# Two transformer blocks on one core: experts' rows leave through DRAM and come back by index on GpSimd

## What is computed

```python
def moe_swiglu(x, w_router, w_gate, w_up, w_down):
    logits = xt @ w_router
    top_vals, top_idx = lax.top_k(logits, 2)
    probs = softmax(top_vals)
    combine = sum(one_hot(top_idx, 8) * probs[..., None], axis=1)
    for e in range(8):
        acc = acc + combine[:, e] * swiglu(xt, w_gate[e], w_up[e], w_down[e])
    return acc

x = layer_norm(ALPHA * x + moe_swiglu(x, ...), ln2_g, ln2_b)
```

## Time and profile before

| | |
|---|---|
| median of 3 runs | 1999.91 us (1999.88 to 2001.02) |
| profiled execution: first to last instruction (span) | 1997.8 us |
| PE busy | 1971.7 us (99%) |
| DVE busy | 1586.5 us (79%) |
| ACT busy | 1226.4 us (61%) |
| POOL busy | 98.7 us (5%) |
| mean granted TensorE clock | 0.998 |
| weights of the experts | 384 transfers of 704 KB |

### The profile page before, as it was taken

How to read it: one execution, slowest core, us unless ns; L and a number is a source line. 1 busy time by engine, 2 the same in 40 slices (tenths; PEclk the granted TensorE clock), 3 DMA queues, 4 the chain that set the end, 5 groups by cost and what they waited for, 6 DMA issues and landing times.

```text
span 1997.8 us, 30577 instructions
## 1 busy us (share of the span) xinstructions
PE 1971.7 (99%) x11807; PEld 1679.3 (84%) x11807; DVE 1586.5 (79%) x1630; ACT 1226.4 (61%) x1323; POOL 98.7 (5%) x163
## 2 busy tenths in 40 slices
PE   8999999999999999999999999999999999999997
PEld 6888888888888898888889888888888888888886
DVE  7787745868774579776658878999999899999997
ACT  6665534566553457455536537777777777777775
POOL 0400000040000000000000000000000000000000
PEclk9999999999999999999999999999999999999999
DMA  8326555632655555075545209999999999999995
GB/s 302 120 90 212 190 190 179 217 117 95 206 190 190 184 201 168 3 236 190 190 169 196 101 19 388 362 362 366 365 358 368 360 366 365 364 364 363 366 361 199
DMA packets 154089, 481.08 MB, mean 241 GB/s; under 512 B 14608, under 2 KB 41728, under 8 KB 153856
## 3 DMA queue, kind: packets, MB, share of 16 engines
q1 hardware_dynamic: 150064, 465.46, 64.7%
q0 software_dynamic: 3920, 14.16, 2.0%
HBM read 477.48 MB, written 2.10 MB: 240 GB/s over the span
## 4 chain that ended last, share of the span: by engine, by line
PE 91%; DVE 6%; ACT 1%; DMA 1%; issue 1%; POOL 1%; SPq 0%; DVEq 0%; POOLq 0%; ACTq 0%
PE G L707 16%; PE G L709 16%; PE G L708 16%; PE Sp L707 5%; PE Sp L709 5%; PE Sp L708 5%; PE G L1212 3%; PE G L734 3%; PE G L1511 3%; PE G L1213 2%; PE G L694 1%; DVE ring_lo L2251 1%; PE G L1512 1%; PE G L689 1%; PE G L690 1%; PE Sp L1212 1%
## 5 line engine op out<-in xcount | busy, mean ns | idle before, releaser
L2174 ACT ACTIVATE e_hi<-e_raw 128x1408 fp32r<-128x1408 f32 x384 | 523.8, 1381 | 156.4 <-DMA e_raw<-in_moe_w_gate 64.2
L3043 DVE TENSOR_TENSOR e_lo<-e_raw,e_hi 128x1408 fp32r<-128x1408 f32 x384 | 601.9, 1620 | 20.1 <-ACT e_hi L2174 17.6
L2251 DVE TENSOR_TENSOR ring_lo<-ring,ring_hi 128x2048 fp32r<-128x2048 f32 (+2 forms) x171 | 383.5, 2254 | 183.2 <-ACT ring_hi L1714 181.8
L1714 ACT ACTIVATE ring_hi<-ring 128x2048 fp32r<-128x2048 f32 (+1 forms) x179 | 335.5, 1883 | 227.5 <-PE G L709 109.7
L707 PE MATMUL G<-e_hi,xgTh 128*128 128x512 f32 (+1 forms) x768 | 289.2, 377 | 0.1
L709 PE MATMUL G<-e_hi,xgTl 128*128 128x512 f32 (+1 forms) x768 | 288.5, 376 | 0.0
L708 PE MATMUL G<-e_lo,xgTh 128*128 128x512 f32 (+1 forms) x768 | 287.1, 374 | 0.0
L708 PEld LDWEIGHTS G<-e_lo,xgTh 128*128 128x128 f32 x768 | 144.2, 188 | 23.9
L709 PEld LDWEIGHTS G<-e_hi,xgTl 128*128 128x128 f32 x768 | 144.0, 188 | 23.0
L707 PEld LDWEIGHTS G<-e_hi,xgTh 128*128 128x128 f32 x768 | 144.3, 188 | 22.7 <-DVE e_lo L3043 0.4
L707 PE MATMUL G<-ring_hi,xT 128*128 128x512 f32 (+2 forms) x360 | 140.4, 390 | 0.0
(11 more groups left out here) (480 smaller groups left out, 3589.9 us busy)
## 6 DMA issues: line engine op xcount, KB each, us to landing
e_raw<-in_moe_w_gate SPq DMA_DIRECT2D x128, 704.0 KB, 6.0
e_raw<-in_moe_w_up SPq DMA_DIRECT2D x128, 704.0 KB, 6.0
e_raw<-in_moe_w_down SPq DMA_DIRECT2D x128, 704.0 KB, 5.9
ring<-in_w_in SPq DMA_DIRECT2D x48, 1024.0 KB, 5.1
ring<-in_w_mlp_up SPq DMA_DIRECT2D x32, 1024.0 KB, 5.2
ring<-in_w_mlp_down SPq DMA_DIRECT2D x32, 1024.0 KB, 4.8
...
```

Source lines behind the costliest of these rows:

```text
L1714: nc.scalar.activation(ring_hi[:, n % H, 0:m], ring[:, n % R, 0:m], ACT.Copy).then_inc(w_hi.sem, 1)
L2174: nc.scalar.activation(e_hi[:, u, :], e_raw[:, u, :], ACT.Copy).then_inc(w_hi.sem, 1)
L2251: v.tensor_tensor(ring_lo[:, n % R, cs], ring[:, n % R, cs], ring_hi[:, n % H, cs].bitcast(F32), ALU.subtract).then_inc(w_lo.sem, 1)
L3043: v.tensor_tensor(e_lo[:, u, :], e_raw[:, u, :], e_hi[:, u, :].bitcast(F32), ALU.subtract).then_inc(w_lo.sem, 1)
```

## The change

PE and DVE no longer bring an expert's result back to the tokens. ACT still copies `Sp` (to `YB`, the same place, plain fp32), and POOL stores the 128 rows to a DRAM tensor `rows_of_y` at row 128 * expert. DVE computes in expert 0, behind unit 24, the rank of each token in each of its two experts (`ranks`); POOL turns that in expert 1 into row numbers (`numbers_of_rows`) and writes `ALPHA * X` to `ACC`. A token whose expert is the last one (7) gets the number of a row of zeros. In the last expert, after its own fetch of tokens (iteration 7 of `expert_pool`), POOL fetches each token's two rows by index (4 indirect DMAs of 128 rows), multiplies each by the token's weight and adds it to `ACC` (`rows_added`, 8 operations on 128 x 1024). DVE waits for that behind its loop. The last expert's rows still go through `YBh`, `YBl` and PE, as before. `scatter`, `result_low`, `add_back` and, in expert 0, `token_of_slot(1)` with its wait go away; the loops over experts remain whole.

```diff
+    YROWS = sb("YROWS", [P, 4 * NTB], U32)
     rows_d = nc.dram_tensor("rows_of_x", (S, D), F32, kind="Internal").ap()
+    Y_ZERO, Y2_ZERO = (NE - 1) * P, NE * P
+    y_d = nc.dram_tensor("rows_of_y", (Y_ZERO + 1, D), F32, kind="Internal").ap()
+    y2_d = nc.dram_tensor("rows_of_later_y", (Y2_ZERO + 1, D), F32, kind="Internal").ap()
...
-        def scatter(tb):
-            for h in range(2):
-                cs = slice(h * 512, (h + 1) * 512)
-                pe.matmul(Sp[:, h, :], PmT[:, tb, :], YBh[:, cs], start=True, stop=False)
-                last = pe.matmul(Sp[:, h, :], PmT[:, tb, :], YBl[:, cs], start=False, stop=True)
-            last.then_inc(m_sc[tb].sem, 1)
-
...
-                if j == 3 and not first:
-                    pe.wait_ge(m_y.sem, i)
-                    scatter(0)
-                if j == KT - 1 and not first:
-                    pe.wait_ge(m_acc.sem, 2 * i + 2)
-                    scatter(1)
-                if first and j == KT:
-                    token_of_slot(1)
                 if j == KT + 4:
                     if not first:
-                        pe.wait_ge(m_acc.sem, 2 * i + 3)
+                        pe.wait_ge(m_yh.sem, i)
                     pe.wait_ge(m_p.sem, i + 2)
                     token_of_slot(0)
                 if j == 2 * KT + 1:
...
-            nc.scalar.activation(YBh[:, :], Sp[:, :, :].rearrange("p b n -> p (b n)"), ACT.Copy).then_inc(m_yh.sem, 1)
+            act.wait_ge(y_stored.sem, n * 16)
+            nc.scalar.activation(YB, Sp[:, :, :].rearrange("p b n -> p (b n)"), ACT.Copy).then_inc(m_yh.sem, 1)
...
+        act.wait_ge(y_stored.sem, n_all * 16)
...
-                do(v.memset(ACC, 0.0), m_acc)
...
-        def add_back(i, tb):
-            dve.wait_ge(m_sc[tb].sem, i)
-            dve.wait_ge(m_acc.sem, i * 2 + (tb + 1))
-            v.scalar_tensor_tensor(ACC[:, tb, :], Sp[:, :, :].rearrange("p b n -> p (b n)"), CW[:, tb, bass.ds(i, 1)], ACC[:, tb, :],
-                                   ALU.mult, ALU.add).then_inc(m_acc.sem, 1)
+        def ranks():
+            do(v.tensor_tensor(RANKED, SELECTED, RK[:, :, 0:8].unsqueeze(1).to_broadcast([P, 2, NTB, NE]), ALU.mult))
+            do(v.tensor_reduce(RANK.rearrange("p (w t) -> p w t", w=2), RANKED, AX_X, ALU.add), y_ranked)
...
-        def result_low():
-            v.tensor_tensor(YBl[:, :], Sp[:, :, :].rearrange("p b n -> p (b n)"), YBh[:, :].bitcast(F32), ALU.subtract).then_inc(m_y.sem, 1)
...
-                if j == DVE_AHEAD and not first:
-                    dve.wait_ge(m_yh.sem, i)
-                    result_low()
...
-                if j == 3 + DVE_AHEAD and not first:
-                    add_back(i, 0)
+                if first and j == 3 * KT:
+                    ranks()
                 if j == KT - 1 + DVE_AHEAD:
-                    if first:
-                        dve.wait_ge(m_i.sem, 1)
-                        do(v.tensor_tensor(SLOTS[:, 0:2], Sp[:, 1, 0:1].to_broadcast([P, 2]), c("less"), ALU.add))
-                    else:
-                        add_back(i, 1)
-                    slots_to_tokens()
+                    if not first:
+                        slots_to_tokens()
                     slots(i + 1)
                 if j == 2 * KT + DVE_AHEAD - 1:
-                    dve.wait_ge(m_i.sem, i + 2)
+                    dve.wait_ge(m_i.sem, i + 1)
...
-        dve.wait_ge(m_acc.sem, n_all * 2 + 1)
-        for tb in range(NTB):
-            do(v.scalar_tensor_tensor(ACC[:, tb, :], X[:, tb, :], ALPHA, ACC[:, tb, :], ALU.mult, ALU.add))
+        dve.wait_ge(y_added.sem, 1)
...
+                for dst, s in ((y_d[Y_ZERO:, :], y_stored), (y2_d[Y2_ZERO:, :], y_zero)):
+                    pool.dma_start(dst.rearrange("o (p n) -> (o p) n", p=P), zeros).then_inc(s.sem, 16)
...
+        def rows_stored(i):
+
+            pool.wait_ge(m_yh.sem, i + 1)
+            dst, b = (y_d, i) if i < NE - 1 else (y2_d, i - (NE - 1))
+            pool.dma_start(dst[b * P:(b + 1) * P, :], YB).then_inc(y_stored.sem, 16)
...
+        def tokens_times_alpha():
+
+            for tb in range(NTB):
+                step(pool, g.tensor_scalar(ACC[:, tb, :], X[:, tb, :], ALPHA, None, ALU.mult), pstep)
...
+        def numbers_of_rows():
+
+            pool.wait_ge(y_ranked.sem, 1)
+            step(pool, g.tensor_scalar(YROW.rearrange("p (w t) -> p w t", w=2), IDXF[:, :, 0:2].rearrange("p t w -> p w t"), float(P), None, ALU.mult), pstep)
+            step(pool, g.tensor_tensor(YROW, YROW, RANK, ALU.add), pstep)
+            step(pool, g.tensor_scalar(YFIRST, RANK, float(P), None, ALU.is_lt), pstep)
+            step(pool, g.tensor_scalar(YTMP, YROW, float(Y_ZERO), float(Y_ZERO), ALU.min, ALU.subtract), pstep)
+            step(pool, g.tensor_tensor(YTMP, YTMP, YFIRST, ALU.mult), pstep)
+            step(pool, g.tensor_scalar(YTMP, YTMP, float(Y_ZERO), None, ALU.add), pstep)
+            step(pool, g.tensor_copy(YROWS[:, 0:2 * NTB], YTMP), pstep)
...
+        def rows_added(src, q0, s, stepped):
+
+            for w_ in range(2):
+                for tb in range(NTB):
+                    q = q0 + w_ * NTB + tb
+                    g.indirect_dma_start(YIN[w_][tb], None, src, bass.IndirectOffsetOnAxis(YROWS[:, q:q + 1], 0)).then_inc(s.sem, 16)
+            pool.wait_ge(s.sem, 16 * 2 * NTB)
+            for w_ in range(2):
+                for tb in range(NTB):
+                    weight = PR[:, tb, 2 + w_:3 + w_].to_broadcast([P, D])
+                    step(pool, g.tensor_tensor(YIN[w_][tb], YIN[w_][tb], weight, ALU.mult), stepped)
+                    last = g.tensor_tensor(ACC[:, tb, :], ACC[:, tb, :], YIN[w_][tb], ALU.add)
+                    if w_ * NTB + tb < 2 * NTB - 1 or q0:
+                        step(pool, last, stepped)
+            if not q0:
+                last.then_inc(y_added.sem, 1)
...
+            if i:
+                rows_stored(i - 1)
             expert_pool(i)
+            if i == 1:
+                tokens_times_alpha()
+                numbers_of_rows()
         pool.wait_ge(m_flag.sem, 1)
...
+            numbers_of_later_rows()
+            pool.wait_ge(y_zero.sem, 16)
+            pool.wait_ge(y_stored.sem, 16 * 2 * NE)
+            rows_added(y2_d, 2 * NTB, y2_in, y2step)
+        pool.wait_ge(y_stored.sem, 16 * NE)
+        rows_added(y_d, 0, y_in, pstep)
```

More of the change, by code:

```diff
@@ L225, in build @@
     mv = small(4).rearrange("p (t n) -> p t n", t=2)
+    zeros = small(D // P)
     def ar(o, n):
@@ L360, in build @@
     ANY = ar(om + 4608 + 296, NTB * NE).rearrange("p (t e) -> p t e", t=NTB)
+    RANKED = ar(om + 4608 + 320, 2 * NTB * NE).rearrange("p (w t e) -> p w t e", w=2, t=NTB)
+    RANK, YROW, YTMP, YFIRST = (ar(om + 4608 + 352 + 2 * NTB * i, 2 * NTB) for i in range(4))
+    YIN = [[XN[:, 0, :], XN[:, 1, :]], [ar(2 * FT2 * S + 2 * HALF + 1024 + tb * D, D) for tb in range(NTB)]]
     ROUTE = G[:, 0:NTB, 0:2 * NE].rearrange("p t (w e) -> p t w e", w=2)
@@ new lines, in numbers_of_later_rows @@
+        def numbers_of_later_rows():
+            step(pool, g.tensor_scalar(YTMP, YROW, float(Y_ZERO), None, ALU.is_ge), y2step)
+            step(pool, g.tensor_tensor(YTMP, YTMP, YFIRST, ALU.mult), y2step)
+            step(pool, g.tensor_scalar(RANK, YROW, float(Y_ZERO + Y2_ZERO), None, ALU.subtract), y2step)
+            step(pool, g.tensor_tensor(YTMP, YTMP, RANK, ALU.mult), y2step)
+            step(pool, g.tensor_scalar(YFIRST, YFIRST, -1.0, 1.0, ALU.mult, ALU.add), y2step)
+            step(pool, g.tensor_scalar(RANK, YROW, float(Y2_ZERO), float(Y2_ZERO), ALU.min, ALU.subtract), y2step)
+            step(pool, g.tensor_tensor(RANK, RANK, YFIRST, ALU.mult), y2step)
+            step(pool, g.tensor_tensor(YTMP, YTMP, RANK, ALU.add), y2step)
+            step(pool, g.tensor_scalar(YTMP, YTMP, float(Y2_ZERO), None, ALU.add), y2step)
+            step(pool, g.tensor_copy(YROWS[:, 2 * NTB:], YTMP), y2step)
```

14 lines of the change are left out of this document (9 added, 5 removed).

## The result

The changed kernel takes **2004.10 us** (median of 13 runs, 2001.98 to 2006.23) where the kernel before, on the same chip, takes 1999.88 (13 runs, 1999.04 to 2001.02): ratio 1.0021, 95% interval 1.0014 to 1.0028. It is slower by 4.2 us, just over the 4.0 us that the prediction took as the least that can be told from no change. The profiled executions stand at spans of 2000.2 and 1997.8 us: +2.4. The profiled execution of the change was its fastest; what its other runs add, up to 4 us, is in no trace, and stays open.

A forecast was written before the change was run, and what follows sets the result against it. PE was taken to bound the stage from expert 1 on. -13.0 - 1.2 + 0.5 + 15 = +1.3 us on the 1997.8 span, median 2.1 above: 2001.2 us; overall range 1986 to 2009.

The forecast's parts named there:

- That PE bounds the stage: From expert 1 on, PE never waits for DVE, ACT or DMA; an expert's matmuls take 96.4 us.
- The scatters, -13.0 us: Experts 1 to 7: 14 scatters of 0.93 us leave PE's path, 13.0 us gained.
- Expert 0, -1.2 us: Expert 0: DVE 1.9 us earlier removes most of PE's wait before its transposes; 1.2 us gained, between 0 and 1.5.
- Nothing for the stores: POOL's 512 KB store per expert costs nothing: 378 GB/s needed, while the stage's first loads moved 410 to 437.
- The last expert, +15 us: Expert 7: POOL's eight operations take turns with DVE's `e_lo`, holding the port 2.28 us each; 15 us lost, between 0 and 23.
- The two lead terms: Expert 7: DVE's lead pays 4 us of the loss, less 2 us taken by the fetches.
- The chain behind, +2: Expert 7: late units make the second `gated_e` late, and PE's transposes behind it: 2 us.
- The tail, 15 us as before: Behind the last down product: the tail should stay as long as before, 15 us.
- the first: Rival, expert 7: the turns cost nothing, by DVE's pauses or arbitration favouring DVE; 1986 us, chance 0.15.
- The second: Rival, expert 7: half is hidden, beside `gated_e` and `hidden_e` or by two DVE units per turn; about 1994 us, chance 0.15.
- The third: Rival, expert 7: hidden values' chain falls on PE's path if POOL's operations pass unit 31; up to 7 us more, chance 0.15.
- the fourth, the full DMA: Rival: DMA is full at 363 GB/s, +1.9 us per expert and 5.8 for the fetches; 2018 us or more, chance 0.05.

The follow-up runs named there:

- the kernel before with the early Silu table: The kernel before, with ACT's Silu table loaded in expert 0 behind the high part of unit 8: 2000.03 us, ratio 0.9998.
- the kernel with early fetches: Changed kernel with its additions on DVE and the four fetches issued at the start of expert 7, behind expert 6's store: 1991.82 us, ratio 0.9956.

## Why the prediction was right, and where it wasn't

The forecast was 2001.2 us and no difference that can be told; it came to 2004.1 and a difference just past that bound, inside the range. Of the 2.9 us between them 1.1 are in the terms: they were to give +1.3 us of span and gave +2.4, made of -12.7, 0.0, 0.0 and +15.3, less 0.2 for an earlier start. The other 1.8 us are in no trace. By its steps:

- **That PE bounds the stage.** Right, but read off the wrong rows: in the order of PE, `w_low_part` is waited for ahead of the first of a unit's three products, L707, not ahead of L708, which thus could never show a wait. The right group says the same (1200 to 1998):

```profile
L707 PE MATMUL G<-e_hi,xgTh 128*128 128x512 f32 x512 | 203.4, 397 | 0.1
```


- **The scatters, -13.0 us.** Right in its mechanism and size: the periods of experts 1 to 6 fell by 1.8 us each, and with neither fetches nor arithmetic expert 7 fell by 1.8 as well: -12.7 in all.
- **Expert 0, -1.2 us.** Wrong: 0.0. The step that failed is "With DVE 1.9 us earlier most of this is gone". DVE was earlier at its wait, and found ACT 2.09 us late instead. ACT's table load of 1.28 us lay beside the wait that was taken away. The kernel before showed it in the timeline of ACT, which the prediction doesn't draw on for this stretch:

```profile
1226.51 1.28 ACT L2178 ACT_TABLE_LOAD   x1
```

  Taken away as well, it gave 1 us.
- **Nothing for the stores.** Right (94.9 us is PE's own pace), but for a reason too weak: that 378 GB/s is needed of 410 to 437 holds on average only. Behind each store all 424 are in use for 20 us. With three more, 2.3 us per expert are lost.
- **Expert 1, +0.5 us.** 0.0. One `e_lo` took 2.45 us instead of 1.61 beside the scaling of `ACC`, within a lead of 2 us.
- **The last expert, +15 us.** 15.3, right in mechanism, and right in its sum partly by luck. The hold per operation was put at 2.28 us and is 1.94 on average (1.69 and 2.20): eight `e_lo` of 27.2 us in all, less 8 x 1.91, are 11.9 us, not 15.1. The two lead terms were the other way. The lead was not 4 us where it counted: in expert 7 with neither fetches nor arithmetic it is 1.0 us at unit 21 and 2.9 at unit 26. And the fetches didn't take 2 us of it but all of it and 2.0 us more, so that no lead paid anything. The chain behind, +2, was 1.4: what is left of 13.3 less 11.9, about PE's stand of 1.52 us before the transposes.
- **The tail, 15 us as before.** Right, and DVE's idle 4.9 us ahead of it were the place where the additions cost 0.3 us and not 13.3. Over all profiled executions the tail lies between 15.0 and 17.7 us, for the additions, for the clock in its eight matmuls (one execution of the kernel before with the early Silu table has it at 16.0), and in part for reasons that no run takes apart.

Of the rivals, the first is out: `e_lo` rows of 3.3 to 3.8 us. The second's mechanism is real (operations beside `gated_e` cost nothing, a part of the step from 13.3 to 9.0 us), but the fetches landed too late for it. The third's condition came true, POOL's operations reached past unit 31 with a lead of 0.1 us, but it cost 1.52 us of waiting and not up to 7. `gated_e` late on PE's path showed again in the kernel with early fetches, with 2.16 us and the clock as a price on top that the prediction had not named. Of the fourth, the full DMA, a share of 2.0 us was there, in the last expert alone.
